# Attention of a hybrid block on one core: score products on array halves, two sets of score banks, fixed slots, and a combination of the two maps shared out by columns

## The reference, cut to what matters

```python
def diff_attention(q, k, v, lam):                 # 128-query blocks
    s = einsum('bqhmd,bkhmd->bhmqk', qblk, k) * dh ** -0.5
    p = softmax(s, axis=-1)
    a = p[:, :, 0] - lam * p[:, :, 1]
    return einsum('bhqk,bkhe->bqhe', a, v)
# latent queries: keys = 512 latent + 128 cached ones; context queries: the 128 context keys
o_d = rmsnorm(o_d, diff_subln_g) * (1.0 - lam_init)
branch_d = o_d.reshape(B, L, DIFF_V_W) @ w_diff_out
```

## Time and profile before

| | us |
|---|---|
| median of 3 runs | 1432.03 |
| lowest, highest | 1429.55, 1432.61 |
| span of the profiled execution | 1432.7 |
| first score matmul | 651.30 |
| start of L1150, after the last output tile | 797.02 |

### The profile page before, as it was taken

One profiled execution on the slowest core, in us unless ns is written; L12 is line 12 of the kernel. 1 busy time (PEld: TensorE's weight loads), 2 busy tenths in 40 slices (PEclk: granted clock), 3 DMA queues, 4 the chain that ended last, 5 costly groups with the idle time before them and its releaser, 6 DMA issues.

```text
span 1432.7 us, 24335 instructions
## 1 busy us (share of the span) xinstructions
PE 1363.0 (95%) x9545; PEld 1291.3 (90%) x9545; DVE 638.5 (45%) x935; ACT 452.0 (32%) x777; POOL 112.9 (8%) x205
## 2 busy tenths in 40 slices
PE   4899999999999999998999899989999999999996
PEld 1699998899999999996777599989999999999996
DVE  3733112466557534645777644352324232333244
ACT  5421313344211122216777522242211122212223
POOL 1011000300111111202111300000000000000000
PEclk9999999999999999999999999999999999999998
DMA  9444231143444343530000014202121212221211
GB/s 303 146 116 118 59 88 44 53 134 116 144 150 137 103 128 101 168 128 30 0 0 0 30 59 147 89 30 88 59 88 61 87 59 88 73 75 61 72 45 73
DMA packets 100820, 127.05 MB, mean 89 GB/s; under 512 B 3433, under 2 KB 91986, under 8 KB 100770
## 3 DMA queue, kind: packets, MB, share of 16 engines
q1 hardware_dynamic: 90624, 95.20, 21.1%
q0 software_dynamic: 8928, 30.09, 6.7%
q10 hardware_dynamic: 1218, 1.07, 0.2%
HBM read 115.34 MB, written 4.72 MB: 84 GB/s over the span
## 4 chain that ended last, share of the span: by engine, by line
PE 88%; DVE 4%; issue 2%; SPq 2%; ACT 2%; POOL 1%; DMA 1%; DVEq 0%; ACTq 0%; POOLq 0%
PE psum L340 49%; PE psum L355 26%; PE psum L760 4%; PE psum L787 2%; PE psum L774 2%; SPq L481 1%; PE psum L321 1%; DVE probs L1359 1%; PE psum L762 1%; PE psum L671 1%; DMA ada_a<-in_w_ada 1%; POOL diag L635 1%; PE psum L388 1%; PE psum L389 1%; PE psum L722 1%
## 5 line engine op out<-in xcount | busy, mean ns | idle before, releaser
L305 DVE TENSOR_TENSOR w_lo<-w_raw,w_hi 128x2048 fp32r<-128x2048 f32 x78 | 178.7, 2291 | 307.8 <-ACT w_hi L300 299.8
L340 PE MATMUL psum<-h_hi,w_lo 128*128 128x320 f32 x1344 | 308.5, 311 | 3.4 <-DVE hf L431 1.4
L340 PE MATMUL psum<-h_hi,w_hi 128*128 128x320 f32 x1344 | 307.4, 310 | 0.0
L340 PE MATMUL psum<-h_lo,w_hi 128*128 128x320 f32 x1344 | 307.2, 310 | 0.0
L340 PEld LDWEIGHTS psum<-h_hi,w_lo 128*128 128x128 f32 x1344 | 225.4, 189 | 4.4 <-issue 4.3
L340 PEld LDWEIGHTS psum<-h_lo,w_hi 128*128 128x128 f32 x1344 | 225.9, 189 | 0.0
L340 PEld LDWEIGHTS psum<-h_hi,w_hi 128*128 128x128 f32 x1344 | 225.7, 189 | 0.0
L300 ACT ACTIVATE w_hi<-w_raw 128x2048 fp32r<-128x2048 f32 x77 | 146.8, 1906 | 149.1 <-PE psum L355 97.7
L355 PE MATMUL psum<-w_lo,h_hi 128*128 128x256 f32 x480 | 136.1, 283 | 0.0
L355 PE MATMUL psum<-w_hi,h_lo 128*128 128x256 f32 x480 | 135.8, 283 | 0.0
L355 PE MATMUL psum<-w_hi,h_hi 128*128 128x256 f32 x480 | 135.8, 283 | 0.0
(11 more groups left out here) (214 smaller groups left out, 1842.6 us busy)
## 6 DMA issues: line engine op xcount, KB each, us to landing
w_raw<-in_w_in SPq DMA_DIRECT2D x32, 1024.0 KB, 5.9
ada_b<-in_w_ada POOLq DMA_DIRECT2D x32, 512.0 KB, 4.1
w_raw<-in_w_ffn_gate SPq DMA_DIRECT2D x11, 1024.0 KB, 5.1
w_raw<-in_w_ffn_up SPq DMA_DIRECT2D x11, 1024.0 KB, 5.1
ada_a<-in_w_ada SPq DMA_DIRECT2D x8, 1024.0 KB, 12.4
w_raw<-in_w_ffn_down SPq DMA_DIRECT2D x8, 1024.0 KB, 5.1
w_raw<-in_w_ret_out SPq DMA_DIRECT2D x4, 1024.0 KB, 5.1
swapped<-qk_d POOLq DMA_DIRECT2D x32, 128.0 KB, 2.5
```

The source lines that it names most:

```text
L305: dve.tensor_tensor(w_lo[s][:, :, :], w_raw[s][:, :, :], w_hi[s][:, :, :].bitcast(F32), ALU.subtract).then_inc(w_lo_done, 1)
L340: last = pe.matmul(bank(4 * par + 2 * j + h, HALF), w[:, k, cs], x[:, k, h * HALF:(h + 1) * HALF], start=(k == 0 and n == 0), stop=(k == K ...
```

## The change

Scores are taken by partition halves: for map m the 64 partitions of `qk_d` of that map go into the matmul directly (in the built program: tile size 64x128 at row 0 or 64), `qz` and GpSimd's copies are gone. One tile's scores of both maps now lie in three banks, and there are two sets of three (banks 0 to 2 for even n, 3 to 5 for odd n); the middle bank of a set holds 128 columns of either map, and `at_shared` orders the two writers. Transposes and outputs share banks 6 and 7: chunks 0 to 3 of the transposes in bank 6, chunk 4 and the output in bank 7. The loops over heads are unrolled to slots: in slot s TensorE does outputs(s-4), weights_T(s-3), scores(s+1); VectorE evacuate_o(s-4), factor(s-1), maximum(s+1); ScalarE evacuate_T(s-3), exp(s). One reduction takes the maximum of both maps. VectorE combines keys 0 to 255, GpSimd keys 256 to 639 in two operations (for the context tile all 128 keys). The output's evacuation and its sum of squares move from ScalarE to VectorE.

```diff
+            def scores(n):
+                h, t = n // TILES, n % TILES
+                b0 = 3 * (n % 2)
+                if n >= 2:
+                    pe.wait_ge(at_e, 2 * n - 2)
+                m0, m1 = slice(0, DHD), slice(DHD, P)
+                q = slice(t * P, (t + 1) * P)
+                k = DH + h
...
+                    pe.matmul(bank(b0 + 1, P), qk_d[m0, h, q], kc_T[m0, h, :], start=True, stop=True).then_inc(at_shared, 1)
+                    pe.matmul(bank(b0 + 2, LAT - P), qk_d[m1, h, q], qk_d[m1, k, P:LAT], start=True, stop=True)
+                    pe.matmul(bank(b0), qk_d[m0, h, q], qk_d[m0, k, 0:LAT], start=True, stop=True)
+                    pe.matmul(bank(b0 + 2, P, LAT - P), qk_d[m1, h, q], kc_T[m1, h, :], start=True, stop=True)
+                    pe.wait_ge(at_shared, n - h + 1)
+                    last = pe.matmul(bank(b0 + 1, P, LAT - P), qk_d[m1, h, q], qk_d[m1, k, 0:P], start=True, stop=True)
...
+                for c in range(keys_of(n) // P):
+                    if c == (DVE_KEYS // P if full else 0):
+                        pe.wait_ge(at_a, n + 1)
+                    if c == LAT_TILES and n >= 1:
+                        pe.wait_ge(at_oe, n)
...
+            for slot in range(-1, QT + 4):
+                if 0 <= slot - 4:
+                    outputs(slot - 4)
+                if 0 <= slot - 3 < QT:
+                    weights_T(slot - 3)
+                if slot + 1 < QT:
+                    scores(slot + 1)
...
+            for n in range(QT):
+                size = keys_of(n)
+                first = DVE_KEYS if size == TOK else 0
+                p0, p1 = probs[:, n % 3, 0, first:size], probs[:, n % 3, 1, first:size]
+                pool.wait_ge(at_f, n + 1)
+                pool.tensor_scalar(p1, p1, sm[:, n % 8, 6:7], None, ALU.mult).then_inc(at_w, 1)
+                pool.wait_ge(at_w, n + 1)
+                pool.tensor_tensor(p0, p0, p1, ALU.add).then_inc(at_a, 1)
...
+            def evacuate_o(n):
...
+                dve.wait_ge(at_o, n + 1)
+                dve.tensor_scalar(out, x, r0, None, ALU.mult).then_inc(at_oc, 1)
+                dve.wait_ge(at_oc, n + 1)
+                dve.scalar_tensor_tensor(junk_o[:, :], x, r0, out, ALU.mult, ALU.mult,
+                                         accum_out=stats[:, n:n + 1]).then_inc(at_oe, 1)
```

More of the change, by code:

```diff
@@ L229, in bank, with scores_at @@
             return psum[:, b * BANK + at_:b * BANK + at_ + n]
+        def scores_at(n, m):
+            first = 3 * (n % 2) * BANK + m * (896 if n % TILES < LAT_TILES else 2 * BANK)
+            return psum[:, first:first + keys_of(n)]
         def T_tile(b):
@@ L766, in scores, with weights_T @@
                 last.then_inc(at_s, 1)
-            def weights_T(h0, t0, first=False):
-                h, t, n = tile_of(h0, t0)
-                pe.wait_ge(at_a, n + 1)
-                if not first:
-                    pe.wait_ge(at_aT, n)
-                for c in range(TILES if t < LAT_TILES else 1):
-                    last = pe.transpose(bank(4 + c // 4, P, (c % 4) * P), probs[:, PBUF[t], 0, c * P:(c + 1) * P], ident[:, :])
+            def weights_T(n):
+                full = keys_of(n) == TOK
+                if full:
+                    pe.wait_ge(at_av, n - n // TILES + 1)
+                if n >= 1:
+                    pe.wait_ge(at_aT, n)
+                for c in range(keys_of(n) // P):
[3 more added lines that the diff above has]
+                        pe.wait_ge(at_oe, n)
+                    last = pe.transpose(bank(6 + c // 4, P, (c % 4) * P), probs[:, n % 3, 0, c * P:(c + 1) * P], ident[:, :])
@@ L775, in weights_T, with outputs @@
                 last.then_inc(at_T, 1)
-            def outputs(h0, t0):
-                h, t, n = tile_of(h0, t0)
+            def outputs(n):
+                h, t = n // TILES, n % TILES
                 pe.wait_ge(at_aT, n + 1)
-                pe.wait_ge(at_oe, n + (2 if t == 0 else 1))
-                out = bank(6 + t % 2, P)
-                for c in range(TILES if t < LAT_TILES else 1):
-                    if t == LAT_TILES:
-                        val = v_d[:, LAT_TILES, bass.ds(h * P, P)]
-                    else:
-                        val = v_d[:, c, bass.ds(h * P, P)] if c < LAT_TILES else v_cache[:, bass.ds(h * P, P)]
-                    last = pe.matmul(out, aT[:, TBUF[t], c, :], val, start=(c == 0),
-                                     stop=(c == LAT_TILES or t == LAT_TILES))
-                last.then_inc(at_o, 1)
@@ L815, in _ @@
-            pe.wait_ge(at_oe, 2 + DH * TILES)
+                if n >= 1:
+                    pe.wait_ge(at_oe, n)
+                hs = slice(h * P, (h + 1) * P)
+                chunks = keys_of(n) // P
+                for c in range(chunks):
+                    val = v_d[:, LAT_TILES, hs] if t == LAT_TILES else v_d[:, c, hs] if c < LAT_TILES else v_cache[:, hs]
+                    last = pe.matmul(bank(7, P, 2 * P), aT[:, n % 3, c, :], val, start=(c == 0), stop=(c == chunks - 1))
+                last.then_inc(at_o, 1)
@@ L1075, in _ @@
+            set_table(ACT.Exp)
+            for slot in range(QT + 3):
+                if slot >= 3:
+                    evacuate_T(slot - 3)
+                if slot < QT:
+                    exp(slot)
+                if slot == QT:
+                    set_table(ACT.Sqrt)
             root("normo", DH * TILES)
@@ L1377, in _, with maximum @@
-            for t in range(2, TILES):
-                if t + 1 < TILES:
-                    maximum(DH - 1, t + 1, 0)
-                weights(DH - 1, t, 0)
-                if t + 1 < TILES:
-                    maximum(DH - 1, t + 1, 1)
-                weights(DH - 1, t, 1)
-            dve.wait_ge(at_oe, 2 + DH * TILES)
+            def maximum(n):
+                dve.wait_ge(at_s, n + 1)
+                at_, apart = 3 * (n % 2) * BANK, (896 if n % TILES < LAT_TILES else 2 * BANK)
+                both = psum[:, at_:at_ + 2 * apart].rearrange("p (m k) -> p m k", m=2)[:, :, 0:keys_of(n)]
+                dve.reduce_max(sm[:, n % 8, 0:2], both, axis=AX.X, negate=True).then_inc(at_max, 1)
@@ L1386, in _ @@
+            for slot in range(-1, QT + 4):
+                if 0 <= slot - 4:
+                    evacuate_o(slot - 4)
+                if 0 <= slot - 1 < QT:
+                    factor(slot - 1)
+                if slot + 1 < QT:
+                    maximum(slot + 1)
+            dve.wait_ge(at_oe, QT)
             mean("normo", DH * TILES, 1.0 / P, RMS_EPS)
```

178 lines of the change are left out of this document (44 added, 134 removed).

## The result

| | before | after |
|---|---|---|
| median of 6 runs, us | 1432.32 | 1442.24 |
| lowest, highest | 1429.08, 1434.29 | 1439.65, 1443.93 |
| span of the profiled execution | 1432.7 | 1439.8 |
| first score matmul | 651.30 | 649.25 |
| last output tile done, mean of squares starts | 797.02 | 802.47 |

The changed kernel is slower by a small amount that is clear of the noise: ratio 1.0057, interval 1.0038 to 1.0077. The forecast was 1442.

What follows compares the result with a forecast made beforehand. TensorE was taken to bound the kernel (busy 1363.0 of 1432.7 us). Seven heads +7.9, filling and emptying +0.8, behind the stage +1.7 sum to +10.4; 1432.0 + 10.4 = 1442 us, range 1428 to 1470.

Steps and rivals of the forecast that it cites:

- The ring: Attention stage, full slot: VectorE's evacuation, TensorE's last transpose and scores, VectorE's maximum wait in a circle, 4.05 us.
- Rival 2: Scores: the array's halves don't run side by side, scores 2.16 us, ring 4.90, in all 1468; chance 0.15.
- rival 3: Scores: fp32 on half a tile needs less streaming, scores under 0.99 us, in all 1419; chance 0.10.
- Rival 1: The ring as short as it can be: 3.62 us, scores 1.08, no tile-change cost, in all 1432; chance 0.20.
- Evacuation 0.72: VectorE's output in the ring: scaled copy 0.29, product with sum of squares 0.34, handing over 0.04 each, row sum 0.06.
- Last transpose: TensorE's step in the ring after VectorE's release: one transpose with its weight load not hidden, 0.22 us.
- the change to half tiles: TensorE in the ring, from whole array to half tiles before the scores: taken as 0.15 us, bounds 0 and 0.30.
- Scores 1.30: TensorE's scores of both maps in the ring, passes starting in program order: 1.30 us, between 1.08 and 2.16.
- The other slots: Two of a head's five slots: 3.05 us where the context tile is transposed, 3.30 where scores and output are its.
- Rival 4: TensorE's clock falls to 1.2 GHz: ring 5.57 us, in all about 1487; chance 0.05.
- The ends: Filling 12.7 and emptying 11.9 us of the attention stage, together 24.6 against 24.1: +0.8 with clock and start adjustments.
- Behind the stage: GpSimd's diagonal products begin 1.8 instead of 2.7 us ahead, one more falls beside VectorE: +1.7 before `o_nat`'s transposes.

Runs made afterwards that it cites:

- the early release: Changed kernel, with bank 7 released after VectorE's scaled copy and the square taken from that copy in SBUF: 1431.49 us, ratio to before 0.9978.
- the halves in turn: Changed kernel, with map 1's score products in full tiles waiting until map 0's are complete: 1500.38 us, ratio to before 1.0465.
- The reordered kernel: Changed kernel with four `probs` buffers, TensorE's scores first, ScalarE's exp before evacuate_T, VectorE's maximum before factor, bank 7 released after the copy: 1442.39 us, ratio 1.0064.

## Why the prediction was right, point by point

**The ring** was the likeliest case, and it is what happens: the waits have its two links, the early release takes its 0.4 out, the halves in turn put 1.38 in, and the evacuation on another engine opens it. Rival 2 (halves not side by side) and rival 3 (less streaming for half a tile) are out: the scores of a tile take 1.29 from their first pass to the first of the outputs (707.12 to 708.41), where rival 2 had 2.16 and rival 3 under 0.99. Rival 1, the shortest ring, had 3.62 and a head of 17.1; the 3.88 and 17.94 lie about midway between it and the forecast.

**Its terms.** Evacuation 0.72 predicted, 0.74 measured, and its parts differ: the copy took 0.34, where the prediction had 0.29 by the reduction. The row sum is a separate small instruction of 0.08, where I took 0.06. Release 0.04 and 0.05. Last transpose 0.22, and then 0.15 for the change to half tiles: together 0.37 predicted, 0.26 measured, so if the transpose is worth its 0.22, what the change to half tiles costs is 0.04 us. Scores 1.30 predicted, 1.29 measured, but not by the steps that were given for it (0.11, 0.32, 0.43, 0.43): the passes of map 0 start at 707.12, 707.33, 707.45 and 707.88 and the outputs at 708.41, so the steps are 0.21, 0.12, 0.43 and 0.53. The last is 0.10 over the pace of such a pass (0.86/2); it stands at the change back to the whole array, and may be its price, which no run isolates. That the sums agree is luck; the hand-over behind them 0.20 and 0.13 (708.41 to 708.54). Maximum 1.42 and 1.41. In all 4.05 against 3.88, with the excess in the change of tile shape, which no row of before showed, and in the hand-over.

The Trainium skill ("TensorEngine Tiling (Array Packing)", section "Key Properties") says that changing the tiling mode drains the engine. The trace doesn't contradict it and gives its price here only as an estimate: 0.04 us going to half tiles, by the 0.22 that I gave the last transpose alone, and at most 0.10 going back, by the pace of a pass.

**The other slots.** 3.05 and 3.30 predicted, 2.96 and 3.34 measured. A head was to be 18.50 and is 17.94 at the full clock, 0.57 more than before, not 1.13: the steps are worth half of what the prediction gave them.

**The clock** is the term that the sum put at nothing in the heads. Rival 4 had it all or nothing: every slot at 1.2 GHz and 1487. What happens lies between, three heads with one slot each largely at the lower level, 3.3 us in all. So seven heads are 128.9 us (661.35 to 790.20), against a forecast of 129.5 and 121.6 before: the ring's 3.9 too much and the clock's 3.3 too little nearly cancel. That the 1442 met the measured time so closely is luck; the direction, the ring and its order are not.

**The ends.** Filling 12.1 (649.25 to 661.35), predicted 12.7. Emptying 12.3 (to 802.47), predicted 11.9. GpSimd's scaling took 1.53 us for 384 columns, at the upper end of 0.5 to 1.5, and as said it costs nothing: the waits view has no wait of TensorE for GpSimd. VectorE's combination, which starts just ahead of that scaling in each slot (707.23 and 707.29), kept its usual 0.48. Beside GpSimd's addition it did not: twice in the filling (660.30 and 662.51) it took 0.66 and 0.92. So the hindrance that the prediction priced at up to 1 us exists, and the order of the slot keeps the two apart in the heads. The reordered kernel, in which an operation on SBUF takes 0.81 beside the addition, shows what it costs otherwise.

**Behind the stage** the forecast was +1.7. From the mean of squares to the first transpose of `o_nat` it took 11.5 (797.02 to 808.50) and now 13.0 (802.47 to 815.43): +1.5. GpSimd starts on `ones` and the diagonal products 2.1 ahead of the mean of squares (800.36; 1.8 was the forecast, 2.7 it was before), and the products take 12.9 us in all, where they took 12.0.

**What was not in the sum.** The stage began 2.05 us earlier, where I had 0.2: 1.9 of it lie in the part of the program ahead of the stage, which the change doesn't touch; the runs of one kernel differ by more. Sum of the profile: -2.05 + 7.5 + 1.5 = +7.0, the spans' difference being 7.1; the medians differ by 9.9 (interval of the ratio: 5.4 to 11.0 us). The 2.8 between them are less than the runs of one kernel differ by.

**Slips in its sums.** None moves the forecast by more than a fraction of a microsecond. VectorE's output comes to 0.73 by its terms, not 0.72. The idle time before the maximum is 1.00 by its own 4.05 less 3.05, where it names 0.8; 0.82 was measured. The two terms behind the stage, 0.9 and 1.0, make 1.9 where it takes 1.7. And rivals 1 and 3 leave out part of the ends: with its own +2.5 they come to 1432.5 and 1421.

## What to carry to other kernels

A change that takes work off the busiest engine can lengthen its waits by more than it takes: ask of each bank that is shared who releases it, what that releaser stands behind on its own engine, and what is queued behind the waiter, and add up the way round. Where such a ring sets the pace, move its cheapest link: here by the ratios, one release moved by one instruction gave 11 us back, and the evacuation given to an engine that isn't in the ring gave 22. And cost TensorE's waits twice, at the full clock and with some slots at half of it, since the same wait was followed by a fall in some heads of a profile and not in others.

## What the runs showed of the hardware

- Products on the two halves of the array overlap, also against the order of the program: the third product started 0.31 us before the second when its half was free. One after another the same products take 2.80 us with the drain, side by side 1.42.
- The granted clock fell to between 0.50 and 0.59 for 2 to 4 us in three heads, though TensorE was busy 81% of a head, and in a head of another kernel in which it was busy 88%. Behind a wait of 1.2 to 2.0 us once a head it fell in 16 of 28 cases over four profiles; where that wait was filled, in none of seven. The same busy time before it (0.35 and 1.63 of 2 us) was followed by a fall once and by none twice.
- VectorE's operation with both operands in SBUF took 0.81 instead of 0.29 us when GpSimd's addition ran beside it, and ended 0.15 behind the addition; in the kernel with the early release it reached 1.10. The form with one operand in PSUM always took 0.35. VectorE's combination that started 0.06 ahead of GpSimd's scaling wasn't lengthened (0.48).
- GpSimd's scaling by a column of factors took 1.53 us for 384 columns, half as much again as its addition of two operands, 1.00.
